# A prologue on one core: sixteen C loads and four B loads issued from the sync queue, angles folded once on VectorE, parameters requested at piece 5

## The chip, the cores and the metric

The kernel runs on one core of a Trainium2 chip. The metric is the device time of one execution in microseconds (us). The core has five engines with a queue each: PE (TensorE, the matrix engine), DVE (VectorE), ACT (ScalarE), POOL (GpSimd) and SP (SyncE, which only issues transfers). ACT and POOL issue transfers too. Engines meet at semaphores.

## The reference

One inference step of a hybrid encoder layer over two groups of tokens: 1024 prompt tokens and 64 sample tokens (1088 in all), model width 2048, all in float32. The input is RMS-normalised and multiplied by `w_in`; the columns feed an S5 branch (64 groups of 16 channels, each driving 64 complex states) and a forgetting-attention branch (8 heads of 128). Both are gated, normalised, concatenated and multiplied by `w_out`. What matters here is the discretisation of the S5 parameters:

```python
dt = exp(log_dt)[:, None]
mag = exp(a_re * dt)
abar_re, abar_im = mag * cos(a_im * dt), mag * sin(a_im * dt)
den = a_re * a_re + a_im * a_im
nr, ni = abar_re - 1.0, abar_im
coef_re, coef_im = (nr * a_re + ni * a_im) / den, (ni * a_re - nr * a_im) / den
bb_re = coef_re * (u @ b_re) - coef_im * (u @ b_im)
bb_im = coef_re * (u @ b_im) + coef_im * (u @ b_re)
# h[t] = abar * h[t-1] + bb[t];  y = c_re . h_re - c_im . h_im + d * u
```

The kernel needs powers 1 to 8 of `abar` and the angles of six further powers, hence 14 multiples of `a_im * dt` for 4096 states: a tile `arg` of 128 x 448, whose cosines and sines go to `trg` (2 x 448 columns).

## The kernel before

It has three parts: a prologue, the S5 part and, after a barrier of all engines, the attention, gate and output part. The change touches the prologue and the start of the S5 part.

**Prologue.** The tokens come as nine tiles `m` = 0 to 8 of 128 rows (the last has 64), 1 MB each. SP loads them (L333, L339); tiles 4 to 8 reuse the place of an earlier one and wait (`X_FREE`) until PE has transposed it (`x_t`). Per tile, ACT squares and sums it in four instructions (`x_square`, L399), DVE reduces the four sums (L568), ACT takes the root (L405), DVE inverts it and scales the tile (L571 to L578), PE transposes it (`tiles`, L960), ACT writes the high part `XH` (`x_split`, L411) and DVE the rest `XL` (`x_rest`, L586). On ACT the order in step m is `x_square(m+1)`, `x_split(m)`; on DVE it is `x_scale(m+1)`, `x_rest(m)`. PE transposes tile m+1 only when `x_rest(m)` has released the PSUM banks. PE also computes the gate columns after tiles 3, 6 and 8 (`gate`, L973), and transposes C after tiles 5 and 6 (`turn_c`, L982; DVE takes it with `take_c`, L593).

ACT's queue also issues transfers: eleven for the parameters at the start, and behind `x_split(m)` of steps 0 to 4 four each: the sixteen `load_c` of 32 KB (L385, rows of 256 bytes) and the four `load_b` of 128 KB (L390, rows of 64 bytes).

POOL works on the parameters in one long chain, each instruction waiting for the one before: `exp_poly` for dt (L783 to L796, 32 columns), the multiples `arg` (L807), the fold of the angles into -pi to pi, once for the cosine and once for the sine (L815 to L825, 10 and 9 instructions of 448 columns), `mag` (L832), `exp_poly` on 256 columns, then, after ACT's sine (L430, `trg_sin`), the packing of `pk` (L840 to L874). L882 stores `pk` to DRAM (`st_pk`).

**Start of the S5 part.** PE streams weight pieces: `w_in` comes in pieces of 256 rows x 128 columns into `wraw` (L167), ACT makes `whi` (L172), DVE makes `wlo` (L176), and PE multiplies each with all tokens in 18 matmuls of three column groups (L188). A column tile of 128 output columns has 8 pieces. ACT and DVE prepare piece s+4 in step s. At step `BEGIN` = 3 both first wait for `st_pk`, DVE clears three tiles (L746 to L748), and ACT then issues the load of the parameters `PJ` of group block 0 (L545). One step later DVE builds `DC` and `BD` (`prepare`, L627 to L632) and half of `Q` (`prepare_q(0)`, L642 to L645), two steps later the other half (L648 to L651). In step 7 (`HP - 1`) DVE and ACT take the finished column tile out of PSUM (`take_u`, L656, L450). POOL builds `GR` from `PJ` (L894 to L899, `g_ready`), which PE must transpose (L1000) before piece 8; after piece 8 PE transposes the tile U (`st1`, L1024), for which it waits for ACT's and DVE's copies `LS` (L459, L666). From there the loop over blocks j runs.

Of the kernel before, what the change touches and what calls it, by code (L numbers as in the profile page):

```python
# [24 lines left out]
NG, GC, NP = 64, 16, 64  # L25
D_PROJ = 2 * D_SSM + 4 * D_ATT + NH
EPS = 1e-6
P = 128
# [18 lines left out]
MAGIC = 12582912.0  # L47
# [3 lines left out]
def build_kernel(nc, x_prompt, x_sample, cache_k, cache_v, cache_logf, state_ssm_re, state_ssm_im,  # L51
# [12 lines left out]
    def sem(name):  # L64
        if name not in sems:
            sems[name] = nc.alloc_semaphore(name=f"{name}_{phase[0]}")
        return sems[name]
# [55 lines left out]
    with ctx:  # L123
# [86 lines left out]
        with ExitStack() as st:  # L210
# [12 lines left out]
            wki = sbp("wki", [P, 256], i32)  # L223
            cf = sbp("cf", [P, 8, 32])
            wg = sbp("wg", [P, KT, 2 * NH], r32)
            pk = sbp("pk", [P, 8, PKW])
# [30 lines left out]
        def x_all(m):  # L257
# [8 lines left out]
        ident_done, par_t, par_ev, dt_bc = sem("ident_done"), sem("par_t"), sem("par_ev"), sem("dt_bc")  # L266
        sq_done, xs_done, x_t, x_hi, x_lo = (sem(n) for n in ("sq_done", "xs_done", "x_t", "x_hi", "x_lo"))
        sqrt_done, ssq_v, trg_in, trg_sin, c_t, c_ev, pk_done = (
            sem(n) for n in ("sqrt_done", "ssq_v", "trg_in", "trg_sin", "c_t", "c_ev", "pk_done"))
# [3 lines left out]
        with ExitStack() as st:  # L273
# [27 lines left out]
            NJ = 8  # L301
            BEGIN = 3
            HP = KT // PIECE
# [26 lines left out]
            with nc.Block() as block:  # L330
                @block.sync
                def _(sp):
                    sp.dma_start(x_all(0), x_prompt[0, 0:P].rearrange("p (k c) -> p k c", k=KT)).then_inc(ld_x[0], 16)  # L333
                    sp.dma_start(gain[:], norm_gain[0:1, :].to_broadcast([P, D_MODEL])).then_inc(ld_gain, 16)
                    for m in range(1, TT):
                        if m in X_FREE:
                            sp.wait_ge(x_t, 4 * (X_FREE[m] + 1))
                        src = x_prompt[0, m * P:(m + 1) * P] if m < TT - 1 else x_sample[0]
                        sp.dma_start(x_all(m), src.rearrange("p (k c) -> p k c", k=KT)).then_inc(ld_x[m], 16)  # L339
                        if m == 1:  # L340
                            sp.dma_start(wf, w_in_v[:, :, D_PROJ - NH:D_PROJ]).then_inc(ld_wf, 16)
# [24 lines left out]
                def _(act):  # L366
# [14 lines left out]

                    def load_c(i):
                        a = (ssm_c_re, ssm_c_im)[i // 8]
                        q, g = i % 8 // 2, i % 2
                        act.dma_start(cin[:, i // 2, g * NP:(g + 1) * NP], a[0].rearrange("(q r g) c p -> q g r c p", q=4, g=2)[q, g]).then_inc(ld_c, 16)  # L385

                    def load_b(i):
                        a = (ssm_b_re, ssm_b_im)[i // 2]
                        g = i % 2
                        act.dma_start(braw[g * NP:(g + 1) * NP, i // 2].rearrange("p (r c) -> p r c", c=GC),  # L390
                                      a[0].rearrange("(r g) p c -> g p r c", g=2)[g]).then_inc(ld_b, 16)
                    act.wait_ge(ident_done, 2)
# [22 lines left out]
                    for m in range(TT):  # L415
                        if m + 1 < TT:
                            x_square(m + 1)
                        x_split(m)
                        if m == 0:
                            act.wait_ge(ld_wf, 16)  # L420
                            S.copy(wg[:, :, 0:NH], wf).then_inc(wg_hi, 1)
                        if m < 5:
                            for i in range(4 * m, 4 * m + 4):
                                if i < 16:
                                    load_c(i)
                                else:
                                    load_b(i - 16)
                        if m == 5:
                            act.wait_ge(trg_in, 1)
                            S.activation(trg[:].rearrange("p a b c -> p (a b c)"),  # L430
                                         trg[:].rearrange("p a b c -> p (a b c)"), ACT.Sin).then_inc(trg_sin, 1)
                        if m == 7:
                            for s in range(SPL):
                                W.split_hi(s, s, 1)
# [125 lines left out]
                def _(dve):  # L560
# [43 lines left out]
                    for m in range(TT):  # L604
# [6 lines left out]
                        if m == 2:  # L611
                            dve.wait_ge(den_in, 1)
                            V.reciprocal(cf[:, 6], cf[:, 2]).then_inc(den_rec, 1)
                        if m == 5:
                            take_c(0)
# [150 lines left out]
                def _(pool):  # L766
                    o = Order(pool, "pool_order")
                    G.memset(epsc[:], EPS)
                    o.then(G.memset(ident[:], 0.0))
                    o.then(G.affine_select(out=ident[:], in_=ident[:], compare_op=ALU.not_equal, fill=1.0, base=0,  # L770
# [37 lines left out]
                    pool.wait_ge(o.sem, last)  # L808

                    argf = arg[:].rearrange("p a b -> p (a b)")  # L810
                    C1, C2, C3 = 6.28125, 1.9350051879882812e-3, 3.0199159819567e-7
                    for i, quarter in ((0, 0.25), (1, 0.0)):
                        t, u = wk[:, 0], wk[:, 1]
                        r = trg[:, i].rearrange("p a b -> p (a b)")
                        o.then(G.tensor_scalar(t, argf, 1.0 / (2 * math.pi), quarter, ALU.mult, ALU.add))  # L815
                        o.then(G.tensor_scalar(t, t, MAGIC, -MAGIC, ALU.add, ALU.add))
                        o.then(G.tensor_scalar(u, t, -C1, None, ALU.mult))
                        o.then(G.tensor_tensor(r, u, argf, ALU.add))
                        o.then(G.tensor_scalar(u, t, -C2, None, ALU.mult))
                        o.then(G.tensor_tensor(r, u, r, ALU.add))  # L820
                        o.then(G.tensor_scalar(u, t, -C3, None, ALU.mult))
                        o.then(G.tensor_tensor(r, u, r, ALU.add))
                        if quarter:
                            o.then(G.tensor_scalar(r, r, math.pi / 2, None, ALU.add))
                        ins = G.tensor_scalar(r, r, -3.1415925, 3.1415925, ALU.max, ALU.min)  # L825
                        if quarter:
                            o.then(ins)
                        else:
                            ins.then_inc(trg_in, 1)
                    pool.wait_ge(trg_in, 1)  # L830
                    for k in range(8):
                        last = o.step(G.tensor_scalar(mag[:, k + 1], ath[:, 0], float(k + 1), None, ALU.mult))  # L832
                    pool.wait_ge(o.sem, last)
                    o.then(G.tensor_copy(xm, mag[:, 1:9].rearrange("p a b -> p (a b)")))
                    exp_poly(mag[:, 1:9].rearrange("p a b -> p (a b)"), xm, 256)
# [1134 lines left out]
```

## Time and profile before

| | |
|---|---|
| median of 3 runs | 2177.96 us (2173.99 to 2178.43) |
| the profiled execution | 2175.9 us, of which the span of the profile is 2174.3 us |
| mean granted TensorE clock | 0.977 of full speed |
| PE busy | 2055.3 us, 95% of the span |
| DVE, ACT, POOL busy | 45%, 33%, 24% |
| prologue: first piece of the weight stream on PE | 94.43 us after the start of the span |
| `st1` transposes of block 0 (L1024), from which the loop runs | 136.53 us |

The page gives busy times and the groups of instructions; the timeline lists instructions in order of time with the idle time of the engine before each and what released it (in brackets); the table of waits sums such idle times by who waited for whom. SPq, ACTq and POOLq are the queues' own instructions, such as issuing a transfer.

### The profile page before, as it was taken

The page shows a single profiled execution, that of the slowest core. Times are in us where ns is not written, and L with a number is a line of the kernel's source. Part 1 is how long each engine was busy: PE and PEld are TensorE (multiplying, and loading weights), DVE is VectorE, ACT ScalarE, POOL GpSimd, SP SyncE. Part 2 cuts the span into 40 slices and gives each one's busy share as a digit, 9 for nine tenths or more (in the row PEclk, how much of TensorE's full clock was granted, in tenths as well). Part 3 has the DMA queues.
Part 4 walks back from the last instruction along what each step waited for, and adds up shares of the span by engine and source line. Part 5 has one row for each costly group of instructions (what it writes and reads, how often), then busy time and mean ns, then how long its engine had stood idle before and what let it go on. Part 6 is the DMA issues. An engine that isn't in the chain of part 4 may idle for free.

```text
span 2174.3 us, 36318 instructions
## 1 busy us (share of the span) xinstructions
PE 2055.3 (95%) x12932; PEld 1966.9 (90%) x12932; DVE 973.6 (45%) x1795; ACT 708.2 (33%) x1458; POOL 519.3 (24%) x771
## 2 busy tenths in 40 slices
PE   4789999999969999999999999999999889999997
PEld 3579999999969999999999999999988879999997
DVE  6454555555533334342524444352564553333332
ACT  5413332333333233333333333334365531111110
POOL 6964555444500001010010101001022212222222
PEclk8799999999989999999999999999999989999999
DMA  6222222222122212112121212112173533333222
GB/s 189 45 68 65 69 69 58 59 69 69 51 57 57 62 32 80 33 43 70 33 81 31 81 31 76 36 44 68 47 265 114 154 98 85 91 87 90 82 84 56
DMA packets 194779, 162.17 MB, mean 75 GB/s; under 512 B 26755, under 2 KB 176429, under 8 KB 193381
## 3 DMA queue, kind: packets, MB, share of 16 engines
q1 hardware_dynamic: 163984, 97.89, 17.2%
q0 software_dynamic: 14704, 51.19, 7.8%
q10 hardware_dynamic: 16036, 12.39, 1.8%
q8 instruction: 31, 0.51, 0.1%
q14 instruction: 24, 0.19, 0.0%
HBM read 124.47 MB, written 36.95 MB: 74 GB/s over the span
## 4 chain that ended last, share of the span: by engine, by line
PE 65%; DMA 2%; DVE 2%; issue 1%; ACT 1%; POOL 0%; SPq 0%; DVEq 0%; POOLq 0%; ACTq 0%
PE GB L188 46%; PE TB L188 9%; PE TB L1781 3%; PE TB L1802 3%; PE TB L1843 1%; PE TB L1826 1%; PE TB L1898 1%; PE TB L1858 1%; DMA ys_s<-QR 1%; DVE QR L1538 0%; DVE QR L1536 0%; DMA out_k_sample<-KO 0%; DMA XL<-ys_s 0%; ACT whi L172 0%; DMA KO<-zs_s 0%
## 5 line engine op out<-in xcount | busy, mean ns | idle before, releaser
L188 PE MATMUL GB<-XH,whi 128*128 128x384 f32 (+1 forms) x2880 | 970.4, 337 | 28.6 <-DVE wlo L176 16.7
L188 PE MATMUL GB<-XH,wlo 128*128 128x384 f32 (+1 forms) x2880 | 947.7, 329 | 0.0
L188 PE MATMUL GB<-XL,whi 128*128 128x384 f32 (+1 forms) x2880 | 945.1, 328 | 0.0
L176 DVE TENSOR_TENSOR wlo<-wraw,whi 128x256 fp32r<-128x256 f32 x544 | 265.9, 490 | 830.1 <-ACT whi L172 826.5
L188 PEld LDWEIGHTS GB<-XH,whi 128*128 128x128 f32 x2880 | 545.8, 190 | 45.0 <-issue 23.6
L188 PEld LDWEIGHTS GB<-XL,whi 128*128 128x128 f32 x2880 | 545.9, 190 | 0.0
L188 PEld LDWEIGHTS GB<-XH,wlo 128*128 128x128 f32 x2880 | 544.7, 189 | 0.0
L172 ACT CAST whi<-wraw 128x256 fp32r<-128x256 f32 x544 | 219.5, 405 | 992.3 <-PE GB L188 811.7
L1247 POOL DMA_DIRECT2D ya_s<-ZR x7 | 4.1, 579 | 750.7 <-DVE ZR L1610 750.7
L1637 DVE RECIPROCAL SQ<-SQ 128x136 f32<-128x136 f32 x128 | 127.7, 997 | 1.1
L188 PE MATMUL TB<-XH,wlo 128*128 128x384 f32 (+1 forms) x384 | 126.0, 328 | 0.0
L188 PE MATMUL TB<-XH,whi 128*128 128x384 f32 (+1 forms) x384 | 125.7, 327 | 0.0
L188 PE MATMUL TB<-XL,whi 128*128 128x384 f32 (+1 forms) x384 | 125.6, 327 | 0.0
L1437 ACT ACTIVATE PR<-PR,nmx 128x128 f32<-128x128 f32 (+8 forms) x72 | 53.4, 742 | 165.2 <-DVE nmx L1623 165.2
L1345 ACT ACT_TABLE_LOAD x64 | 82.1, 1283 | 1.1
L1781 PE MATMUL TB<-PT,VT 128*128 128x128 f32 x576 | 74.7, 275 | 0.7 <-ACT PT L1447 0.7
L1781 PEld LDWEIGHTS TB<-PT,VT 128*128 128x128 f32 x576 | 71.3, 191 | 1.3 <-ACT PT L1447 1.2
L1802 PE MATMUL TB<-KN,QN 128*128 128x512 f32 (+2 forms) x192 | 72.5, 486 | 0.0
L188 PEld LDWEIGHTS TB<-XH,whi 128*128 128x128 f32 x384 | 72.1, 188 | 0.1
L188 PEld LDWEIGHTS TB<-XH,wlo 128*128 128x128 f32 x384 | 72.2, 188 | 0.0
L188 PEld LDWEIGHTS TB<-XL,whi 128*128 128x128 f32 x384 | 72.1, 188 | 0.0
L1621 DVE CUSTOM_DVE_ANT_0 PR<-TB,NCB 128x128 f32<-128x128 f32 (+8 forms) x72 | 51.2, 711 | 39.4 <-PE TB L1803 35.9
(389 smaller groups left out, 2182.7 us busy)
## 6 DMA issues: line engine op xcount, KB each, us to landing
wraw<-in_w_in SPq DMA_DIRECT2D x384, 128.0 KB, 2.2
wraw<-in_w_out SPq DMA_DIRECT2D x128, 128.0 KB, 2.2
xt<-in_x_prompt SPq DMA_DIRECT2D x5, 1024.0 KB, 5.0
NCB<-nc_s POOLq DMA_DIRECT2D x8, 608.0 KB, 5.3
zg_s<-U ACTq DMA_DIRECT2D x8, 544.0 KB, 2.8
XL<-zg_s SPq DMA_DIRECT2D x8, 544.0 KB, 4.6
VR<-zg_s POOLq DMA_DIRECT2D x8, 544.0 KB, 4.6
KO<-zs_s POOLq DMA_DIRECT2D x8, 544.0 KB, 5.9
```

What stands on the lines that cost most here:

```text
L172: S.copy(whi[:, s % SPL], wraw[:, s % RAW]).then_inc(self.hi, 1)
L176: V.tensor_tensor(wlo[:, s % SPL], wraw[:, s % RAW], whi[:, s % SPL].bitcast(f32), ALU.subtract).then_inc(self.lo, 1)
L188: ins = T.matmul(group(GB if bank is None else bank, b), w[:, s % SPL, kk], x[:, k + kk, c:c + n], start=first and kk == 0 and i == 0, sto ...
L1345: o.then(S.activation(tabs[:], epsc[:], func))
L1437: S.activation(PR[0:n, 0:w], PR[0:n, 0:w], ACT.Exp, bias=nmx[0:n], accum_out=rsum[0:n]).then_inc(e["exp"], 1)
L1621: o.then(V.tensor_tensor_reduce(out=PR[0:n, 0:w], in0=TB[0:n, 0:w], in1=NCB[0:n, c:c + w], scale=1.0, scalar=-3e38, op0=ALU.add, op1=ALU.m ...
L1637: o.then(V.reciprocal(a, a))
L1781: ins = T.matmul(O, VT[:, b], PT[:, b * P:(b + 1) * P], start=b == 0, stop=b == i)
L1802: T.matmul(TB[:, c:c + cw], q, KN[:, c:c + cw], start=True, stop=c + cw < w)
L1826: ins = T.transpose(TB[:, 1024 + b * P:1024 + (b + 1) * P], PR[:, b * P:(b + 1) * P], ident[:])
L1843: ins = T.matmul(TB[:, d:d + n], ones[:], SQ[:, c:c + n], start=True, stop=True)
L1858: ins = T.transpose(TB[0:n, d:d + P], src[:, m * P:m * P + n], ident[:])
```

## The change

- `load_c` and `load_b` move from ACT's queue to SP's: C loads 0 to 7 in front of the load of tile 4, 8 to 15 in front of tile 5, the four B loads in front of tile 6.
- POOL no longer folds the angles. It signals `arg_done` after L807, computes `mag` and then waits for DVE's fold (`trg_in`). DVE folds once, in six instructions of 448 columns, behind `x_rest(3)`.
- In step 5 ACT takes the absolute value of the folded angle and then the cosine as sin(pi/2 - |angle|), and the sine, in three instructions where there was one of 896 columns. A new constant `halfpi` is set by POOL.
- `BEGIN` goes from 3 to 5.

```diff
-            BEGIN = 3
+            BEGIN = 5
@@ sync queue
+                    (load_c and load_b as on ACT's queue before, with sp.dma_start)
                     for m in range(1, TT):
+                        if m in (4, 5):
+                            for i in range(8 * (m - 4), 8 * (m - 3)):
+                                load_c(i)
+                        if m == 6:
+                            for i in range(4):
+                                load_b(i)
                         if m in X_FREE:
                             sp.wait_ge(x_t, 4 * (X_FREE[m] + 1))
@@ scalar queue
-                        if m < 5:
-                            for i in range(4 * m, 4 * m + 4):
-                                if i < 16:
-                                    load_c(i)
-                                else:
-                                    load_b(i - 16)
                         if m == 5:
                             act.wait_ge(trg_in, 1)
-                            S.activation(trg[:].rearrange("p a b c -> p (a b c)"),
-                                         trg[:].rearrange("p a b c -> p (a b c)"), ACT.Sin).then_inc(trg_sin, 1)
+                            tf = lambda i: trg[:, i].rearrange("p a b -> p (a b)")
+                            S.activation(tf(0), tf(1), ACT.Abs).then_inc(trg_abs, 1)
+                            act.wait_ge(trg_abs, 1)
+                            S.activation(tf(0), tf(0), ACT.Sin, bias=halfpi[:], scale=-1.0)
+                            S.activation(tf(1), tf(1), ACT.Sin).then_inc(trg_sin, 1)
@@ vector queue, behind x_rest(m)
+                        if m == 3:
+                            dve.wait_ge(arg_done, 1)
+                            argf = arg[:].rearrange("p a b -> p (a b)")
+                            t, r = trg[:, 0].rearrange("p a b -> p (a b)"), trg[:, 1].rearrange("p a b -> p (a b)")
+                            o.then(V.tensor_scalar(t, argf, 1.0 / (2 * math.pi), MAGIC, ALU.mult, ALU.add))
+                            o.then(V.tensor_scalar(t, t, -MAGIC, None, ALU.add))
+                            o.then(V.scalar_tensor_tensor(r, t, -6.28125, argf, ALU.mult, ALU.add))
+                            o.then(V.scalar_tensor_tensor(r, t, -1.9350051879882812e-3, r, ALU.mult, ALU.add))
+                            o.then(V.scalar_tensor_tensor(r, t, -3.0199159819567e-7, r, ALU.mult, ALU.add))
+                            V.tensor_scalar(r, r, -3.1415925, 3.1415925, ALU.max, ALU.min).then_inc(trg_in, 1)
@@ gpsimd queue
+                    G.memset(halfpi[:], math.pi / 2)
@@
-                    (the two folds, L810 to L829)
-                    pool.wait_ge(trg_in, 1)
+                    pool.sem_inc(arg_done, 1)
                     for k in range(8):
                         last = o.step(G.tensor_scalar(mag[:, k + 1], ath[:, 0], float(k + 1), None, ALU.mult))
                     pool.wait_ge(o.sem, last)
+                    pool.wait_ge(trg_in, 1)
                     o.then(G.tensor_copy(xm, mag[:, 1:9].rearrange("p a b -> p (a b)")))
```

## Rows read from the trace of the kernel before

**Rows 1.** The page: busy us, share of the span and instructions by engine.

```profile
PE 2055.3 (95%) x12932; PEld 1966.9 (90%) x12932; DVE 973.6 (45%) x1795; ACT 708.2 (33%) x1458; POOL 519.3 (24%) x771
```

**Rows 2.** PE's waits, 0 to 150 us: total, times, longest.

```profile
PE TB L960 <- DVE XL L586: 28.8, 7, 7.8
...
PE GB L188 <- DVE wlo L176: 4.2, 1, 4.2
```

**Rows 3.** ACT's waits, 0 to 150 us.

```profile
ACT TB L399 <- issue: 12.0, 5, 6.3
```

**Rows 4.** Timeline of DVE in the prologue: start, length, instruction, idle before it.

```profile
26.17 0.16 DVE L568 TENSOR_REDUCE ssq<-ssq 128x1 f32<-128x4 f32 x1 [2.77 <-ACT TB L399]
...
29.83 2.48 DVE L586 TENSOR_TENSOR XL<-TB,XH 128x512 fp32r<-128x512 f32 x4
...
47.67 0.15 DVE L568 TENSOR_REDUCE ssq<-ssq 128x1 f32<-128x4 f32 x1
...
59.50 0.16 DVE L568 TENSOR_REDUCE ssq<-ssq 128x1 f32<-128x4 f32 x1 [5.05 <-ACT TB L399]
...
71.06 0.16 DVE L568 TENSOR_REDUCE ssq<-ssq 128x1 f32<-128x4 f32 x1 [3.70 <-ACT TB L399]
```

**Rows 5.** Timeline of ACT and its queue in the prologue.

```profile
20.92 0.30 ACT L421 CAST wg<-pk 128x128 fp32r<-128x128 f32 x1
...
49.22 3.99 ACTq L390 DMA_DIRECT2D braw<-in_ssm_b_re  x1
...
56.48 0.60 ACT L399 ACTIVATE TB<-XHF 128x512 f32<-128x512 f32 x1 [6.31 <-issue]
...
62.03 1.28 ACT L430 ACT_TABLE_LOAD   x1
67.20 0.95 ACT L430 ACTIVATE trg<-trg 128x896 f32<-128x896 f32 x1 [3.89 <-POOL trg L825]
```

**Rows 6.** Timeline of POOL: multiples of the angle, `mag`, end of the packing.

```profile
30.81 6.40 POOL L807 TENSOR_SCALAR arg<-ath 128x32 f32<-128x32 f32 x14
...
67.25 2.63 POOL L832 TENSOR_SCALAR mag<-ath 128x32 f32<-128x32 f32 x8
...
109.98 1.29 POOL L874 TENSOR_TENSOR pk<-wk,trg 128x512 f32<-128x512 f32 x1
```

**Rows 7.** Timeline of SP's queue.

```profile
3.07 8.33 SPq L339 DMA_DIRECT2D XHF<-in_x_prompt  x1
11.44 2.06 SPq L339 DMA_DIRECT2D XLF<-in_x_prompt  x1
```

**Rows 8.** The view of one tile: issue of C loads (ns min/median/max).

```profile
L385 ACTq DMA_DIRECT2D XLF<-in_ssm_c_im x8: 602/603/1295, 34.2 to 42.9; - x8
```

**Rows 9.** The view of tile xt: issue to landing of its six loads.

```profile
DMA to landing us min/median/max: 4.8/5.3/10.3
```

**Rows 10.** Timeline of PE: tile 4 behind the gate, and the start of the stream.

```profile
46.11 2.36 PE L960 MATMUL TB<-ident,xt 128*128 128x128 f32 x16
...
94.43 0.34 PE L188 MATMUL GB<-XH,whi 128*128 128x384 f32 x1
...
129.46 1.97 PE L1000 MATMUL TB<-ident,M 128*128 128x128 f32 x8 [5.26 <-POOL M L899]
...
136.53 0.27 PE L1024 MATMUL TB<-ident,UZ 128*128 128x128 f32 x1
```

**Rows 11.** Timeline of DVE at the start of the stream.

```profile
117.42 0.15 DVE L746 MEMSET UC<- 128x112 f32 x1 [12.08 <-DMA pk_s<-pk]
...
120.40 0.45 DVE L627 COPY DC<-PJ 128x548 f32<-128x548 f32 x1 [0.50 <-DMA PJ<-pk_s]
...
134.62 0.68 DVE L666 COPY LS<-TB 128x512 f32<-128x512 f32 x1
```

**Rows 12.** Timeline of DVE: durations of instructions on 548 columns.

```profile
157.12 0.72 DVE L698 TENSOR_TENSOR SS<-M 128x548 f32<-128x548 f32 x1
...
179.60 0.42 DVE L627 COPY DC<-PJ 128x548 f32<-128x548 f32 x1
```

More of the change, by code:

```diff
@@ L224, in build_kernel @@
             cf = sbp("cf", [P, 8, 32])
+            halfpi = sbp("halfpi", [P, 1])
             wg = sbp("wg", [P, KT, 2 * NH], r32)
@@ L267, in build_kernel @@
         sq_done, xs_done, x_t, x_hi, x_lo = (sem(n) for n in ("sq_done", "xs_done", "x_t", "x_hi", "x_lo"))
+        arg_done, trg_abs = sem("arg_done"), sem("trg_abs")
         sqrt_done, ssq_v, trg_in, trg_sin, c_t, c_ev, pk_done = (
@@ L334, in _, with load_c, load_b @@
                     sp.dma_start(gain[:], norm_gain[0:1, :].to_broadcast([P, D_MODEL])).then_inc(ld_gain, 16)
-                    for m in range(1, TT):
+                    def load_c(i):
+                        a = (ssm_c_re, ssm_c_im)[i // 8]
+                        q, g = i % 8 // 2, i % 2
+                        sp.dma_start(cin[:, i // 2, g * NP:(g + 1) * NP], a[0].rearrange("(q r g) c p -> q g r c p", q=4, g=2)[q, g]).then_inc(ld_c, 16)
+                    def load_b(i):
+                        a = (ssm_b_re, ssm_b_im)[i // 2]
+                        g = i % 2
+                        sp.dma_start(braw[g * NP:(g + 1) * NP, i // 2].rearrange("p (r c) -> p r c", c=GC),
+                                      a[0].rearrange("(r g) p c -> g p r c", g=2)[g]).then_inc(ld_b, 16)
+                    for m in range(1, TT):
+                        if m in (4, 5):
[4 more added lines that the diff above has]
+                                load_b(i)
                         if m in X_FREE:
@@ L380, in _ @@
                     act.dma_start(vin[33:34], k_norm_gain).then_inc(ld_par, 16)
[L382 to L391, printed above, removed]
                     act.wait_ge(ident_done, 2)
@@ L808, in _ @@
                     pool.wait_ge(o.sem, last)
[L810 to L829, printed above, removed]
-                    pool.wait_ge(trg_in, 1)
+                    pool.sem_inc(arg_done, 1)
                     for k in range(8):
```

## Prediction

> **What bounds the kernel now.** I read the page first: PE is busy 95% of the span [rows 1], nearly all of it the matmuls L188, which this change doesn't touch. So only time in which PE stands still, or does little, can be won, and the change can move that only in the first 140 us. There I read PE's waits [rows 2]: 28.8 us in seven waits for DVE's `XL` in the prologue, and 4.2 for `wlo` after the stream has begun; PE then waits 5.26 for POOL's `GR` [rows 10]. The prologue ends where the first piece starts, at 94.43, and the loop is entered at `st1`, at 136.53 [rows 10]. Everything behind `st1` is a stream that PE feeds itself; I take its length as unchanged. The question is thus by how much `st1` comes earlier.
>
> What sets the prologue's pace is a ring: DVE reduces tile m+1, scales it, makes `XL` of tile m; ACT meanwhile takes the root, splits tile m and squares tile m+2. Write t(m) for the start of the reduce of tile m. DVE alone needs 29.83 + 2.48 - 26.17 = 6.14 a tile [rows 4]. ACT needs 2.53 from the reduce to the end of the split (59.50 to 62.03) and 3.02 for the squares (56.48 to 59.50) [rows 4, 5], 5.55 together, so DVE should be the slower one. But the steps really took longer: t(5) 47.67, t(6) 59.50, t(7) 71.06 [rows 4]. ACT's waits say why: 12.0 us in five places behind "issue" [rows 3], the largest being 6.31 ahead of the squares of tile 6, behind the B loads [rows 5], and 3.89 before the sine, for POOL's fold [rows 5]. DVE's idle times before the reduces, 2.77, 5.05 and 3.70, are the same delays seen from its side [rows 4].
>
> **The change, part by part.**
>
> *Loads leave ACT.* ACT is free of tile 0 and `wg` at 20.92 + 0.30 = 21.2 [rows 5]; it squares tile 2 at once: t(2) = 21.2 + 3.1 = 24.3 (before 26.17). Then DVE's 6.14 rules: t(3) = 30.4, t(4) = 36.6 (a small reciprocal in step 2 is left out).
>
> *Loads on SP.* Twenty issues now stand in front of loads of tokens. SP has issued tile 3 at 13.5 [rows 7]. At 0.60 each [rows 8] C loads 0 to 7 take until 18.3, ahead of the time at which tile 4 may be asked for (20.4, when tile 0 has been transposed). C loads 8 to 15 follow, 20.8 to 25.6; tile 5 is issued at 25.6 and lands 5.3 later [rows 9], at 31. Its squares are due behind the split of tile 3, at t(4) + 2.5 = 39.1: covered with 8 us to spare. The four B loads took ACT's queue 7.9 us in all, the second one 3.99 [rows 5]; on SP, 26 to 34. Tile 6 is issued at 34 and lands by 39.3, or by 44.3 with the longest landing, 10.3 [rows 9]. It is due at t(5) + 2.5 = 48.6. So I cost the moved issues at nothing; the cover is 4 to 9 us. The bound from the other side: at 1.30 a C load, the longest one [rows 8], tile 5 lands at about 40 (1 late), tile 6 at 52 (3 late). Tiles 7 and 8 are asked for when tiles 4 and 5 are transposed, as before, and rows of C and B no longer stand near them.
>
> *The fold.* POOL has the multiples ready at 30.81 + 6.40 = 37.2 [rows 6]; DVE comes to the fold behind `x_rest(3)`, at t(4) + 6.1 = 42.7, so it waits for nothing. Six instructions of 448 columns: three with one tensor, priced 0.42, and three with two, priced 0.72 [rows 12]; both rows are of 548 columns and I leave the surplus for the six hand-overs. 3.4 us; the bounds are 2.8 (scaled to 448 columns) and 5.0 (all at 0.72, and 0.1 for each hand-over). Queued behind it on DVE: the reduce of tile 5, so the whole 3.4 lies on the ring. t(5) = 42.7 + 3.4 = 46.1 (before 47.67). PE transposes tile 4 behind the gate columns, 2.2 earlier than its 46.11 [rows 10], which is early enough for the split. t(6) = 46.1 + 6.1 + 0.5 = 52.7 (before 59.50); the 0.5 is for POOL's `exp_poly`, which now runs beside it.
>
> *Sine and cosine.* In step 5 ACT waits no more (fold ready 46.1). It does root and split (2.5), the absolute value (0.6 with its hand-over), the table load (1.28), two sines of 448 columns (1.1; one of 896 took 0.95) and the squares of tile 7 (3.0) [rows 4, 5]: t(7) = 52.7 + 8.5 = 61.2 against 71.06. ACT sets this step; DVE would need 6.1 + 0.7 for `take_c`. From t(7) to the first piece nothing changes, 94.43 - 71.06 = 23.4 [rows 4, 10]: the stream starts at 84.6, 9.8 earlier.
>
> A rule of the Trainium skill bears on the absolute value: "ScalarE: Activation LUTs", section "Table sets: the hidden batching unit", says that cheap functions, abs among them, are in every table set. By it no further load appears; no row here shows the absolute value, and one more load would cost 1.28, the length of the one in the row [rows 5], and put the stream at 85.9.
>
> *POOL's chain.* Without the folds it has `mag` done at 37.2 + 2.6 = 39.8 and waits for DVE until 46.1. From there to the end of `pk` it has what stood between 67.25 + 2.63 = 69.9 and 109.98 + 1.29 = 111.3, 41.4 us [rows 6]: 87.5. The sine is there at 58, long before. The store took from 111.3 to 117.4 [rows 6, 11]: `st_pk` at 93.6, while the stream reaches step 5 of its preparation five pieces after its start. A piece takes 2.98 us (the matmuls of the stream before the stall ran at that pace, as 94.43 plus eight times 2.98 plus the 4.2 wait and a slow restart of 1.7 give 124.2, 5.26 before 129.46) [rows 2, 10]. DVE clears at 84.6 + 14.9 + 1.3 = 100.8; the wait for `st_pk` has vanished with 7 us to spare, and with it the 4.2 and the slow restart.
>
> *BEGIN = 5.* But now `PJ` is asked for at 100.8, by choice and not by need. It is there 120.40 - 117.42 = 3.0 later [rows 11], 103.8. POOL made `GR` in 129.46 - 120.40 = 9.1 [rows 10, 11]; DVE was at work beside it, which it now is only for the second half, so 8.0 to 9.1, I take 8.5: 112.3. PE has finished piece 7 at 84.6 + 23.9 = 108.5: it waits 3.8 for `GR`. It transposes it (1.6) and multiplies piece 8 (3.9, with a cold start): 117.8. DVE starts `prepare` behind `wlo` of piece 10, at 106.4. Before, it went from 120.40 to 134.62 + 0.68 = 135.3, 14.9 us, from there to its copy of `LS` [rows 11], two `wlo` more than now: 14.0, bounds 10.5 (its copies unhindered by POOL) and 14.9. `LS` is ready at 120.4, and `st1`, which waits for both, starts at 120.4 against 136.53: 16.1 us earlier. `take_u` now stands ahead of the second half of `Q`, which removes the wait for it in piece 8, and `LS` behind it becomes what is late: 2.6 us.
>
> The sum: 9.8 from the prologue, 6.3 from the start of the stream, 16.1. The profiled execution took 2175.9, 2.1 below the median of 2177.96 and within the spread of the runs: 2175.9 - 16.1 = 2159.8, or 2161.9 from the median. I say 2161.
>
> **Rivals.**
>
> *Tokens late (2).* C at 1.3 an issue and a fold at 5.0 cost 3 + 1.6, and if DVE's preparation stays at its upper bound 1 more: 16.1 - 5.6 = 10.5 gained, 2166. The margins of 4 to 9 us speak against it.
>
> *The queue fills (slower).* SP was held 8.33 us by one load of tokens behind four others [rows 7]. If each B load holds SP that long, in front of tile 6, four take 33.3. With C at 1.3 tile 6 is issued at 35 + 33.3 = 68.3 and lands at 73.6; t(6) = 76.6, the stream starts at 76.6 + 8.5 + 23.4 = 108.5, `st1` at 144.3, 7.8 later: 2185. It decides from t(6) = 68.6 on (52.7 + 16.1), that is if tile 6 is issued after 60.3. For it: SP's row. Against: the same four loads took ACT 7.9 us while tokens were moving too. The Trainium skill, "DMA: Bandwidth & Descriptors", section "Queues, rings and completion order", has a rule against the move: an engine takes descriptors of one ring in order and goes round robin between rings. By it the load of tile 6 has all of B before it, where on ACT's ring B ran beside tokens; no row here shows the two orders apart, and it would only lengthen the landing that I bounded at 10.3.
>
> *Only the start is won (the change doesn't do what it says).* If ACT's "issue" idle is not the transfers' but that of something which stays, or the fold on DVE costs the ring what ACT gains, the stream starts where it did. Then only the 6.3 remain: 2171; with 2 us of further waits in the loop, no measurable change, 2175. Against: the five places are exactly the five steps with loads.
>
> **How the numbers follow.** Forecast 0.66 (gain 13 to 19, the upper end from DVE's 10.5 and a `GR` in 8.0), tokens late 0.13, only the start 0.14 (half of it under the bound), slower 0.07. About 0.2%, 4.4 us, can be told from no change. Faster 0.86, same 0.07, slower 0.07. The range takes the first two cases, most of the third and the spread of the runs: 2155 to 2172.
>
> **What would show it.** After: no "issue" idle before L399; t(5) near 46 and t(6) near 53; the six folds within 3.4; two sines and one table load; first piece of the stream near 84.6; no wait for `st_pk`; a wait of about 4 for `GR` and one of 2 to 3 for `LS`; `st1` near 120. It is wrong if SP's B loads take over 15 us, if a tile's squares wait for its load, if DVE waits for `arg_done`, or if the loop behind `st1` grows.

## The result, and the profile after

The changed kernel takes 2159.81 us (median of 4 runs, 2158.79 to 2160.54) against 2177.52 of the kernel before (4 runs): the ratio is 0.9924, with a 95% interval of 0.9908 to 0.9939. The profiled execution took 2158.79 us with a span of 2157.2, against 2175.9 and 2174.3, so 17.1 us less. Forecast were 16.1 less, 2161 us. Run once more on another occasion, beside other kernels, the changed kernel took 2161.5 (ratio 0.9929, 0.9916 to 0.9943).

PE's matmuls are the same, as the page shows (busy us, share, instructions):

```profile
PE 2056.0 (95%) x12932; PEld 1967.2 (91%) x12932; DVE 972.2 (45%) x1801; ACT 708.6 (33%) x1460; POOL 494.3 (23%) x753
```

PE's waits of the changed kernel, 0 to 160 us, answer to [rows 2]. The seven waits for `XL` of 28.8 us are six of 18.9, the one for `wlo` is gone, and what is left at the start of the stream is 2.9 for `GR`, 0.8 for `take_u` and 0.2 in front of `st1`:

```profile
PE TB L956 <- DVE XL L591: 18.9, 6, 4.6
...
PE TB L996 <- POOL M L895: 2.9, 1, 2.9
...
PE GB L188 <- DVE UZ L671: 0.8, 1, 0.8
```

The ring on DVE, from its timeline, answers to [rows 4]. The reduces are t(2), t(3), t(4), t(5), t(6) and t(7); between t(4) and t(5) lie the fold's first and last instruction:

```profile
23.95 0.16 DVE L573 TENSOR_REDUCE ssq<-ssq 128x1 f32<-128x4 f32 x1 [0.53 <-ACT TB L407]
...
30.09 0.14 DVE L573 TENSOR_REDUCE ssq<-ssq 128x1 f32<-128x4 f32 x1
...
36.47 0.10 DVE L573 TENSOR_REDUCE ssq<-ssq 128x1 f32<-128x4 f32 x1
...
42.48 0.38 DVE L623 TENSOR_SCALAR trg<-arg 128x448 f32<-128x448 f32 x1
...
45.30 0.39 DVE L628 TENSOR_SCALAR trg<-trg 128x448 f32<-128x448 f32 x1
...
45.61 0.15 DVE L573 TENSOR_REDUCE ssq<-ssq 128x1 f32<-128x4 f32 x1
...
51.82 0.15 DVE L573 TENSOR_REDUCE ssq<-ssq 128x1 f32<-128x4 f32 x1
...
60.17 0.16 DVE L573 TENSOR_REDUCE ssq<-ssq 128x1 f32<-128x4 f32 x1 [1.45 <-ACT TB L407]
```

DVE sets the pace nearly everywhere: it is idle before only two of these reduces, 0.5 and 1.5 us, where it had been idle before five of the six, for 2.8, 0.3, 1.6, 5.1 and 3.7. The stretches up to t(6) are 6.1 to 6.4 long, but for the one with the fold, 9.14; the last, 8.35, is set by ACT.

ACT in step 5, in its timeline: absolute value, table load, cosine, sine, then at once the squares of tile 7. This answers to [rows 5], where ACT had waited 3.89 us after the table load:

```profile
54.24 0.58 ACT L433 ACTIVATE trg<-trg 128x448 f32<-128x448 f32 x1
54.84 1.28 ACT L435 ACT_TABLE_LOAD   x1
56.13 0.67 ACT L435 ACTIVATE trg<-trg,halfpi 128x448 f32<-128x448 f32 x1
56.70 0.56 ACT L436 ACTIVATE trg<-trg 128x448 f32<-128x448 f32 x1
```

SP's queue, with the moved loads in it. The rows answer to [rows 7] and to the B loads of [rows 5]:

```profile
13.89 7.75 SPq L340 DMA_DIRECT2D XLF<-in_ssm_c_re  x8
21.68 0.45 SPq L357 DMA_DIRECT2D xt<-in_x_prompt  x1
22.18 6.05 SPq L340 DMA_DIRECT2D XLF<-in_ssm_c_im  x8
28.27 0.45 SPq L357 DMA_DIRECT2D xt<-in_x_prompt  x1
28.76 4.40 SPq L345 DMA_DIRECT2D braw<-in_ssm_b_re  x2
33.20 3.15 SPq L345 DMA_DIRECT2D braw<-in_ssm_b_im  x2
36.40 1.51 SPq L357 DMA_DIRECT2D XHF<-in_x_prompt  x1
```

PE's timeline at the start of the stream, which answers to [rows 10]: the first piece at 83.92 instead of 94.43, the transposes of `GR`, and `st1` at 118.65 instead of 136.53:

```profile
83.92 0.34 PE L188 MATMUL GB<-XH,whi 128*128 128x384 f32 x1
...
110.83 1.10 PE L996 MATMUL TB<-ident,M 128*128 128x128 f32 x8 [2.92 <-POOL M L895]
...
118.65 0.35 PE L1020 MATMUL TB<-ident,UZ 128*128 128x128 f32 x1 [0.22 <-issue]
```

So 10.5 us are won in front of the stream and 7.4 between its first piece and `st1` (34.7 instead of 42.1), 17.9 in all; the span is shorter by 17.1. The rest of 0.8 lies behind `st1`: from there to the end of the span the kernel before takes 2037.8 us and the changed one 2038.6. The thirteen profiled executions of this document take between 2036.7 and 2042.4 us for that stretch, so 0.8 is not a change that can be told.

### The profile page after: what moved, and what is told of

Read it like the earlier page. It is cut to its first block, busy times and chain, and to the rows that moved or that the text cites. A ratio compares the mean times of both kernels' runs of the same rounds, so it can differ in the third digit from the quotient of the medians.

```text
span 2157.2 us, 36310 instructions
## 1 busy us (share of the span) xinstructions
PE 2056.0 (95%) x12932; PEld 1967.2 (91%) x12932; DVE 972.2 (45%) x1801; ACT 708.6 (33%) x1460; POOL 494.3 (23%) x753
## 4 chain that ended last, share of the span: by engine, by line
PE 65%; DVE 2%; DMA 2%; issue 1%; ACT 1%; POOL 0%; SPq 0%; DVEq 0%; POOLq 0%; ACTq 0%
PE GB L188 45%; PE TB L188 9%; PE TB L1777 3%; PE TB L1798 3%; PE TB L1839 1%; PE TB L1822 1%; PE TB L1894 1%; DMA ys_s<-QR 1%; PE TB L1854 1%; DMA out_k_sample<-KO 0%; DVE QR L1534 0%; DVE QR L1532 0%; DMA XL<-ys_s 0%; DMA KO<-zs_s 0%; ACT whi L172 0%
## 5 line engine op out<-in xcount | busy, mean ns | idle before, releaser
L188 PE MATMUL GB<-XH,whi 128*128 128x384 f32 (+1 forms) x2880 | 968.3, 336 | 24.6 <-DVE wlo L176 12.0
L188 PE MATMUL GB<-XH,wlo 128*128 128x384 f32 (+1 forms) x2880 | 946.7, 329 | 0.0
L188 PE MATMUL GB<-XL,whi 128*128 128x384 f32 (+1 forms) x2880 | 943.8, 328 | 0.0
L188 PEld LDWEIGHTS GB<-XH,whi 128*128 128x128 f32 x2880 | 544.9, 189 | 40.7 <-issue 24.1
L188 PEld LDWEIGHTS GB<-XL,whi 128*128 128x128 f32 x2880 | 545.1, 189 | 0.0
L188 PEld LDWEIGHTS GB<-XH,wlo 128*128 128x128 f32 x2880 | 544.0, 189 | 0.0
L188 PE MATMUL TB<-XH,wlo 128*128 128x384 f32 (+1 forms) x384 | 125.8, 328 | 0.0
L188 PE MATMUL TB<-XH,whi 128*128 128x384 f32 (+1 forms) x384 | 125.6, 327 | 0.0
L188 PE MATMUL TB<-XL,whi 128*128 128x384 f32 (+1 forms) x384 | 125.5, 327 | 0.0
L188 PEld LDWEIGHTS TB<-XH,whi 128*128 128x128 f32 x384 | 72.1, 188 | 0.1
L188 PEld LDWEIGHTS TB<-XH,wlo 128*128 128x128 f32 x384 | 72.1, 188 | 0.0
L188 PEld LDWEIGHTS TB<-XL,whi 128*128 128x128 f32 x384 | 72.0, 188 | 0.0
```

Of the source, the lines that this page charges most:

```text
L188: ins = T.matmul(group(GB if bank is None else bank, b), w[:, s % SPL, kk], x[:, k + kk, c:c + n], start=first and kk == 0 and i == 0, sto ...
```

## The experiments

In what follows two figures stand for each kernel: the start of the stream (first matmul L188) and how long after it `st1` begins, both from its profiled execution, and the median of its runs. Kernel before: 94.4, 42.1, 2177.5. Changed: 83.9, 34.7, 2159.8. The seven profiled executions whose prologue is that of the changed kernel start the stream at 83.9 to 85.1, so a difference of 1 us there is not read as an effect; the distance to `st1` is 34.73 and 34.70 in the two executions of the changed kernel.

### One part alone: the loads

`e1_loads_only` is the kernel before with this part of the change only:

```diff
@@ scalar queue, step m
-                        if m < 5:
-                            (four of load_c or load_b)
@@ sync queue
+                        if m in (4, 5):
+                            for i in range(8 * (m - 4), 8 * (m - 3)):
+                                load_c(i)
+                        if m == 6:
+                            for i in range(4):
+                                load_b(i)
```

> The kernel before with one part of the change alone: C and B loads on SP. POOL still folds the angles, the sine is one instruction, BEGIN is 3. Theory (the prologue is a ring with due times, and the steps of ACT have two delays one behind the other): t(5) near 43 and t(6) near 50, both about 5 to 9 us earlier than the 47.7 and 59.5 of before, but in step 5 ACT then waits for POOL's fold, which ends near 67 as before, so t(7) is 71 and the stream starts at 94 again: time 2176 within 2 us, ACT's wait for POOL's fold grown from 3.9 to 11 to 14 us. Rival (the parts add up, each its own share of the 17 us): the 12.0 us of issue idle are what is won, the stream starts at 86 to 88 and the time is 2166 to 2169.

Measured: 2177.38 us, ratio 1.0 (0.999 to 1.001). The stream starts at 96.8 and `st1` at 136.2, 39.4 later. The ring is as early as the theory says up to t(6), and then loses it all, as DVE's timeline shows (t(4) to t(7)):

```profile
36.56 0.10 DVE L568 TENSOR_REDUCE ssq<-ssq 128x1 f32<-128x4 f32 x1
...
43.07 0.14 DVE L568 TENSOR_REDUCE ssq<-ssq 128x1 f32<-128x4 f32 x1
...
50.45 0.16 DVE L568 TENSOR_REDUCE ssq<-ssq 128x1 f32<-128x4 f32 x1 [1.25 <-ACT TB L405]
...
71.82 0.16 DVE L568 TENSOR_REDUCE ssq<-ssq 128x1 f32<-128x4 f32 x1 [14.64 <-ACT TB L405]
```

ACT's waits name the cause: the "issue" idle before the squares, 12.0 us [rows 3], does not appear any more, and what had been 3.9 for POOL's fold is now

```profile
ACT trg L430 <- POOL trg L825: 13.7, 1, 13.7
```

The parts do not add up; the loads alone are worth nothing. One thing I had not foreseen: the stream starts 2.4 us later than in the kernel before, though t(7) is only 0.8 later. PE's longest wait for `XL` was 11.5 us instead of 7.8, and its granted clock in the last gate columns (the 7 us before the stream) was 0.63, where it had been 0.76 in the last 6 us of the kernel before. That the lower clock is the whole of the difference was not tried.

### One part alone: the fold

`e2_fold_only` is the kernel before with the fold on DVE, the absolute value and the two sines; the loads stay on ACT and `BEGIN` is 3. Seen from the changed kernel:

```diff
-            BEGIN = 5
+            BEGIN = 3
@@ load_c and load_b back on ACT's queue, behind x_split(m), four a step
```

> The kernel before with the fold on DVE, the absolute value and two sines, and nothing else: loads on ACT, BEGIN 3. Theory: the prologue gains nothing, since the 3.1 us of fold lie on the ring and ACT's issue stays (t(7) near 71, stream at 94.5), but POOL is done with the parameters near 92 and not at 111, so the store is there before step 3 asks for it: the wait of 4.2 for wlo and the one of 5.3 for GR go, PE waits for take_u instead, 1 to 3 us; st1 near 125.5 against 136.5. Time 2165, 10 to 12 us faster. Rival (parts add up by the cost of what each removes on its own engine): POOL's 30 us are off the path of PE and the 3.1 us of DVE are on it, time 2176 to 2181.

Measured: 2163.2 us, ratio 0.9937 (0.9918 to 0.9956). The stream starts at 91.2 and `st1` comes at 123.5, 32.3 later; PE's waits for `wlo` and `GR` are gone, and 2.8 for `take_u` is in their place. The rival is out: POOL's fold did not stand on PE's path by its own 30 us, but the parameters that waited for it did. The theory missed one thing, and it is the 3 us by which the prologue did get shorter. The fold on DVE lay partly in time in which DVE had waited for ACT, and ACT's 3.9 for POOL was gone. DVE's idle times show it:

```profile
49.27 0.15 DVE L573 TENSOR_REDUCE ssq<-ssq 128x1 f32<-128x4 f32 x1
...
59.16 0.16 DVE L573 TENSOR_REDUCE ssq<-ssq 128x1 f32<-128x4 f32 x1 [3.60 <-ACT TB L401]
...
67.51 0.16 DVE L573 TENSOR_REDUCE ssq<-ssq 128x1 f32<-128x4 f32 x1 [1.09 <-ACT TB L401]
```

t(5) is later by 1.6 than in the kernel before, not by the 3.1 of the fold, and the idle time before t(6) fell from 5.05 to 3.60: the loads' issue hid the rest.

### One part alone: BEGIN

`e3_begin_only` is the kernel before with this line changed:

```diff
-            BEGIN = 3
+            BEGIN = 5
```

> The kernel before with BEGIN at 5. Theory: the store of the parameters lands at 117.4 as before, so PJ and GR come as before (GR at 129.5); PE has one piece more ready and does not wait for wlo, but it can't pass piece 8 without GR; take_u stands earlier in DVE's order. st1 near 134.5, 1 to 3 us earlier, time 2174 to 2176. Rival (BEGIN is what makes the gain at the start of the stream, 7 us): st1 near 129.5, time 2169.

Measured: 2176.1 us, ratio 0.9993 (0.9984 to 1.0003): no change that could be told. `st1` starts at 135.1, 1.4 earlier than before, as the theory has it, and 40.8 behind the stream's 94.4. PE's two waits have become one, as long as both and the third for `take_u` together (4.2, 5.3 and 1.4 before):

```profile
PE TB L1000 <- POOL M L899: 11.1, 1, 11.1
```

The sum of the three parts alone is 0 + 14 + 1 us by the medians; together they bring 17 to 18. What the loads are worth once the fold has left POOL is more than the remaining 3. `e4_begin3`, which follows, is `e2_fold_only` with the loads on SP and nothing else changed: 2158.03 us against 2163.2, so 5.2 less, with the first piece at 85.1 against 91.2 and `st1` at 117.7 against 123.5. `BEGIN` = 5, on the other hand, is worth 1 us alone and costs 2 us at `st1` beside the other two.

### BEGIN in the changed kernel

`e4_begin3` and `e5_begin4` are the changed kernel with only this line changed to 3 and to 4:

```diff
-            BEGIN = 5
+            BEGIN = 3
```

> The changed kernel with BEGIN back at 3. Theory: the store has landed at 96.8, while step 3 comes at 94: PJ is asked for at 97.1 instead of 100.2, GR is ready near 109 (DVE works beside POOL all the time), PE waits about 1 us for it and 2 to 3 for take_u; st1 near 116.8 against 118.65, time 2157, 1 to 2 us faster than the changed kernel. Rival (waiting for the store two pieces earlier holds ACT and DVE back, which is why BEGIN was moved): pieces 7 to 9 are late again, st1 at 122 to 125, time 2163 to 2166.

> The changed kernel with BEGIN at 4. Measured from the first piece of the stream, st1 came 34.7 us later in the changed kernel (BEGIN 5) and 32.6 with BEGIN 3. Theory (what is last is DVE's order: the whole of Q stands ahead of take_u as soon as BEGIN is below 5, and it starts 3 us later than with BEGIN 3): GR is ready when piece 7 ends, PE waits under 1 us for it, but 3.5 to 5 for take_u; st1 34 to 35 behind the first piece, time as that of the changed kernel within 1 us. Rival (what counts is only how early the parameters are asked for, and each step is worth the same): halfway between, 33.6, PE's waits in sum between 3.7 and 4.0.

Measured: with 3, 2158.03 us (ratio 0.9908, 0.9889 to 0.9928), `st1` 32.6 behind the first piece; with 4, 2159.93 (0.9917, 0.99 to 0.9933), 34.7 behind it. The medians are too near each other to rank; the traces do it. With 3, DVE waits 3.1 us for the store, which holds PE nowhere; PE waits 1.1 for `GR` and 2.9 for `take_u`; with 4 it waits for `take_u` alone, and that is the longest wait of the three kernels:

```profile
PE GB L188 <- DVE UZ L671: 5.0, 1, 5.0
```

So moving the request to step 5 was not needed once POOL was early, and what is last at this place is the order of DVE's work and not the time of the request: 3 is better by 2.1 us than 5, while 4 is no better.

### Is the fold on the ring? It is doubled

`e6_fold_twice` is the changed kernel with five of the six instructions done twice:

```diff
                             o.then(V.scalar_tensor_tensor(r, t, -3.0199159819567e-7, r, ALU.mult, ALU.add))
+                            (the same five instructions once more)
                             V.tensor_scalar(r, r, -3.1415925, 3.1415925, ALU.max, ALU.min).then_inc(trg_in, 1)
```

> The changed kernel with five of the six fold instructions on DVE done twice, one pass behind the other, 2.85 us more by their durations in the changed kernel's trace. Theory (the fold lies on the ring in full): t(5), t(7) and the first piece of the stream 2.8 later, time 2162.5, 2.5 to 3 us slower than the changed kernel. Rival (DVE has slack there, ACT or a load being late anyway): under 1 us.

Measured: 2162.12 us (ratio 0.993, 0.9913 to 0.9946), 2.3 over the changed kernel. From t(4) to t(5) it takes 11.98 us (36.67 to 48.65) against 9.14: 2.84 more on the ring, where the five instructions last 2.65 and their hand-overs the rest. The first piece starts at 87.4, against 83.9 to 85.1 without the second fold. The fold is paid in full on the ring; that the time grew by as much is likely, but its runs (2160.07 to 2166.03) overlap with those of the changed kernel.

### How much cover has the place in SP's queue?

`e7_all_ahead` is the changed kernel with all twenty loads in front of tile 4:

```diff
-                        if m in (4, 5):
-                            for i in range(8 * (m - 4), 8 * (m - 3)):
-                                load_c(i)
-                        if m == 6:
-                            for i in range(4):
-                                load_b(i)
+                        if m == 4:
+                            for i in range(16):
+                                load_c(i)
+                            for i in range(4):
+                                load_b(i)
```

> The changed kernel with all sixteen C and four B loads ahead of the load of tile 4 on SP. Theory (SP's order costs nothing only while a tile lands before its squares are due; B holds SP some 7.5 us and the tile behind it lands late): tile 4 is issued near 36 and lands near 45, its squares were due at 32.7, so t(4) moves from 36.5 to 48, tile 5 is less late than that, and from there the ring runs as before: stream at 94 to 96, time 2170 to 2172, 11 us slower than the changed kernel. Rival (the DMA engines have room and the place in SP's queue matters little): t(4) within 2 us of the changed kernel's, time 2160 to 2162.

Measured: 2164.82 us (ratio 0.9941, 0.9925 to 0.9958), 5.0 slower than the changed kernel, half of what was expected. Now ACT waits for a tile, 5.5 us, and the ring is late from t(4) on by 4.8 (ACT's wait, and t(4) on DVE):

```profile
ACT TB L406 <- DMA xt<-in_x_prompt: 5.5, 1, 5.5
```

```profile
41.26 0.16 DVE L572 TENSOR_REDUCE ssq<-ssq 128x1 f32<-128x4 f32 x1 [4.57 <-ACT TB L406]
```

The mechanism is there, the size was off, and SP's queue says where: the four B loads held it 4.9 us and not 7.5, so that tile 4 was issued at 32.05 and not at 36, and it was squared from 38.2 on, 6.2 us after its issue and not 9:

```profile
27.04 2.07 SPq L345 DMA_DIRECT2D braw<-in_ssm_b_re  x2
29.15 2.85 SPq L345 DMA_DIRECT2D braw<-in_ssm_b_im  x2
```

In the changed kernel a tile of 1 MB had been issued just ahead of the B loads; here only C loads of 32 KB stood ahead. That the megabyte is what makes the difference was not tried by itself.

### A better order

`e8_q_behind` is the changed kernel with `BEGIN` 3 and the second half of `Q` behind `take_u`:

```diff
-            BEGIN = 5
+            BEGIN = 3
@@ vector queue
-                        if s == BEGIN + 2:
+                        if s == HP - 1:
                             prepare_q(1)
```

> The changed kernel with BEGIN 3 and the second half of Q moved behind take_u on DVE, as BEGIN 5 has it by its place. Theory: PE's wait of 2.9 for take_u with BEGIN 3 goes to under 0.5, then LS is last by under 1 us; st1 31 to 31.5 behind the first piece (32.6 with BEGIN 3 alone, 34.7 in the changed kernel), time 2156 to 2157, the fastest of all. Rival (DVE's work is the same in sum, and LS comes behind all of it): the wait moves from take_u to LS and st1 stays at 32.5, time 2158.

Measured: 2157.14 us (ratio 0.9911, 0.9895 to 0.9928). The wait for `take_u` is gone and `st1` comes 31.4 behind the first piece, where `BEGIN` = 3 alone had 32.6; the medians of these two (2157.14 and 2158.03) are too near each other to rank. What is left ahead of `st1` is 1.8 for `LS` (the profile calls it issue; DVE's copy of `LS` ends just before):

```profile
109.77 1.09 PE L996 MATMUL TB<-ident,M 128*128 128x128 f32 x8 [1.53 <-POOL M L895]
...
115.67 0.35 PE L1020 MATMUL TB<-ident,UZ 128*128 128x128 f32 x1 [1.76 <-issue]
```

`e9_bd_on_act` adds one edit: the four copies of `BD` for block 0 go to ACT.

```diff
@@ scalar queue, behind split_hi of step BEGIN + 1
+                        if s == BEGIN + 1:
+                            act.wait_ge(e["pj_in"], 16)
+                            act.wait_ge(e["zero_done"], 3)
+                            for i in range(2):
+                                for g in range(2):
+                                    ins = S.copy(BD[i * NP:(i + 1) * NP, g::2, g * GC:(g + 1) * GC],
+                                                 bc_(i)[g * NP:(g + 1) * NP])
+                            ins.then_inc(e["bd_ready"], 1)
@@ vector queue
-                            prepare(0)
+                            prepare(0, bd=False)
```

It ran on one chip beside the changed kernel and `e8_q_behind`, each once more (`e11_q_behind_again` has the edit of `e8_q_behind`):

> The kernel with BEGIN 3 and the second half of Q behind take_u, and in addition the four copies that make BD for block 0 given to ACT, which waits at that place. Theory: DVE's way from PJ to LS is last there by 1.8 us, and the four small copies cost it 3.4 us because POOL works beside it; without them LS is ready before PE needs it, PE waits only for GR, 1 to 1.5 us; st1 29.3 to 30 behind the first piece of the stream (31.4 without this, 34.7 in the changed kernel), time 2155 to 2156. Rival (POOL and DVE only take turns: what DVE saves, POOL's GR or ACT's whi loses): st1 31 to 32, time 2157.

> The changed kernel once more, beside the two others, so that they are compared on one chip: 2158.5 to 2160.5.

> The kernel with BEGIN 3 and the second half of Q behind take_u once more: by its trace 2.5 to 3.3 us faster than the changed kernel on the same chip (st1 31.4 instead of 34.7 behind the first piece), 2156 to 2157.5; if the difference is under 1 us, what is won at st1 is given back in the loop.

Measured: 2154.91 (2153.3 to 2157.76; ratio 0.9905, 0.989 to 0.992), 2161.5 for the changed kernel (2158.79 to 2162.77) and 2155.96 for `e11_q_behind_again` (2153.56 to 2156.02; 0.9902, 0.9887 to 0.9917). The runs of the two new ones don't overlap with those of the changed kernel: 5.5 and 6.6 us faster (`e11_q_behind_again` and `e9_bd_on_act`). Of that the traces place 3.2 and 4.6 between the first piece and `st1`. The changed kernel itself came out 1 us above what was expected of it. Between the profiled executions of `e10_changed_again` and `e11_q_behind_again` all but 0.1 of the 5.5 us has a place: 0.55 in front of the stream, 3.2 up to `st1`, and 1.6 in the first 12 us behind `st1`, where PE's granted clock was low in the one and not in the other (see the last section). Of the 8.2 between the profiled executions of `e10_changed_again` and `e9_bd_on_act`, 1.7 lie further back and have no place. The two new ones cannot be ranked against each other. By the trace `BD` on ACT brings 1.4 us (30.1 against 31.5); PE still waits 1.3 for `GR` and 0.7 for `LS`. The expected 29.3 to 30 was just missed, because DVE did not save the 3.4: freed of the copies, its next instructions ran into POOL's. These rows of that kernel show it. In `e11_q_behind_again` the first of the products took 0.76, the second already 1.67, and the two `wlo` together 0.78. So 0.77 and 1.85 of the 3.4 came back; from `DC` to the end of `LS` DVE needed 14.0 us instead of 14.9. In the changed kernel the two products took 0.76 and 0.75; POOL was done with `GR` when they came:

```profile
101.12 1.53 DVE L667 TENSOR_TENSOR UC<-PJ 128x576 f32<-128x576 f32 x1
...
102.58 1.66 DVE L668 TENSOR_TENSOR UCS<-PJ 128x576 f32<-128x576 f32 x1
...
107.62 2.63 DVE L176 TENSOR_TENSOR wlo<-wraw,whi 128x256 fp32r<-128x256 f32 x2
```

## Why the prediction was right, point by point

- **The ring and its two stallers.** Forecast t(2) to t(7): 24.3, 30.4, 36.6, 46.1, 52.7, 61.2. Measured: 23.95, 30.09, 36.47, 45.61, 51.82, 60.17. The 6.14 a tile held. That ACT's "issue" idle was the loads' is shown by `e1_loads_only`, where it disappears with them; so the third rival's first half is out. That both stallers lay one behind the other, so that neither part alone could bring the 9.8, is shown by `e1_loads_only` (first piece 2.4 later), `e2_fold_only` (3.2 earlier) and `e4_begin3` (the two together, 9.3 earlier). The prediction worked both out together and did not say it.
- **Loads on SP at nothing.** The issue took longer than I said: C 7.75 and 6.05 us for eight instead of 4.8, so tile 5 was issued at 28.3 and not 25.6, and tile 6 at 36.4 and not 34. The cover of 4 to 9 us took that up: ACT waited for none of these tiles. The landing of tile 6 took 8.0 us from its issue, and 7.1 to 7.5 in the other eight profiled executions with this order; in the three with B on ACT's queue it took 6.9, 6.4 and 6.2. The rule that I quoted from the Trainium skill, "DMA: Bandwidth & Descriptors", section "Queues, rings and completion order", points the same way as these landings. That it is their cause is not shown, since the time counts from the start of the issue and the issue itself was 1.0 longer (1.51 against 0.55 in the kernel before). `e7_all_ahead` shows that the cover is real and what comes behind it, at a smaller price than I put on it. The slower rival had SP held 8.3 by each B load; held it was 7.5 by all four.
- **The fold.** 3.4 forecast. Six instructions took 3.04 by their durations, and from the first to the following reduce 3.13. `e6_fold_twice` shows it on the ring in full. On the ring the stretch became longer by 3.0 (9.14 against 6.14), between the bound of 2.8 from scaling the rows to 448 columns and the price I took.
- **Sine and cosine.** Forecast 8.5 from t(6) to t(7), measured 8.35. No table load came with the absolute value; the row goes from it straight to the load for the sine. By the Trainium skill, "ScalarE: Activation LUTs", section "Table sets: the hidden batching unit", abs is in every set; the trace agrees for the one set that was loaded then.
- **First piece.** Forecast 84.6, measured 83.9, and 85.0 in the repeated execution. In the first t(7) was 1.0 earlier than forecast, and the stretch behind it, which I had left as it was at 23.4, took 23.75.
- **POOL's chain.** Forecast end of `pk` 87.5; it was at 90.6. The term mis-sized is the stretch behind the fold, 41.4 forecast, 44.8 measured: four instructions of that stretch took over 2 us, where there had been two such in the kernel before; one product took 2.83 against 0.72 for its likes. That DVE's large instructions hold them is how I read it, and the rows fit closely: each of the four starts while DVE scales a tile (2.35 us) and ends 0.3 or 0.6 after that instruction, as if the most part of its usual 0.41 or 0.73 came behind it. No run takes the scaling away from them, so the cause is read and not tested. It cost nothing: the store was issued at 90.95 and, at 5.8 us to land, was there 3 us ahead of DVE's step 5 at 99.9.
- **BEGIN = 5.** Forecast: a wait of 3.8 for `GR` (2.9 measured), and `st1` 35.8 behind the first piece (34.7). The term mis-sized is DVE's way from `prepare` to `LS`, 14.0 forecast, 12.7 measured (105.84 to 118.55): POOL was done with `GR` at 110.8, and behind that the second product for `Q` took 0.75 and the pair that makes `Q` 1.52, where they had taken 1.66 and 3.27 beside POOL in the kernel before. `GR` itself, 8.5 forecast with a lower bound of 8.0, took 7.3 (103.46 to 110.78); with `BEGIN` = 3, where DVE's products for `Q` run beside it, it took 9.0 (101.00 to 109.97 in `e11_q_behind_again`). That this is what ends last I said, with PE's wait of 2.6 before it; in the profiled execution the wait was 0.2, in the repeated one 1.9, with the same 34.7. The difference is piece 8, priced at 3.9, which took 6.7 in the profiled execution at a granted clock of 0.56, with 0.8 for `take_u` in it. PE ended it at 118.43 and `LS` was ready at 118.55. That DVE was still last there is luck by 0.1 us, since the forecast had PE done 2.6 earlier.

The sum was 1.8 too small at `st1` and 1.0 in the profiled time. What the prediction did not weigh is whether the request at step 5 was needed at all. It said that it comes "by choice and not by need" and then priced what is there; `e4_begin3` and `e8_q_behind` show that 2 to 3 us were left there at `st1`.

## What to carry to other kernels

Where several engines pass a tile round in a ring, write down when each step is due and find every staller before pricing any: of two that stand one behind the other, taking one away can be worth nothing, and then be worth much once the other is gone (the loads: 0 us alone, 5.2 with the fold off POOL). Price a part in the kernel that has the others, and not by what the sum leaves over. A transfer's issue is cheapest in a queue that has slack before its next due time, and that slack can be measured by putting more in front. When a chain has become earlier, look again at the step at which its result is asked for, and at the order of work on the engine that ends last there: that was worth 3 us at `st1` for two lines, 2.7 by the medians in one comparison and 5.5 in the other.

## What the runs showed of the hardware

**The same loads hold a queue for different times.** Eight C loads of 32 KB took SP 7.75 and 6.05 us in the changed kernel though their median issue is 0.6; the view of the tile has the longest one:

```profile
L340 SPq DMA_DIRECT2D XLF<-in_ssm_c_re x8: 598/598/3224, 13.9 to 21.0; - x8
```

The four B loads held SP 7.5 us behind a tile of 1 MB (7.4 to 8.0 in the other eight executions with this order) and 4.9 behind C loads, which is one execution.

**A low clock that cost nothing in one execution and 1.6 us in another.** After the wait for `GR` the granted clock was 0.56 of full speed, mostly its lower level of 1.2 GHz, in the profiled execution of the changed kernel all through piece 8, and at its higher one in the repeated execution (stretch, length, busy us of PE, its weight loads, DVE, ACT and POOL, granted clock, transfers):

```profile
111.00:118.70 7.70, 6.67 (x27) 5.83 (x26) 7.36 (x11) 0.82 (x2) 6.83 (x19) 0.56 0.07 17
```

```profile
111.00:118.70 7.70, 4.30 (x26) 3.74 (x26) 7.51 (x11) 1.06 (x3) 6.84 (x16) 1.00 0.07 17
```

`st1` came 34.7 us behind the first piece in both, since DVE's `LS` was what ended last: the slow matmuls filled time in which PE would have waited. But in the repeated execution, where PE was busy for 4.3 of the 7.7 us at the higher level, the low one came 1 us behind `st1`, where PE has no wait to fill: granted clock 0.66 in the first 5 us, against 0.99 in the first execution (the columns as above):

```profile
118.65:123.65 5.00, 5.00 (x38) 4.63 (x42) 1.70 (x3) 1.29 (x4) 4.22 (x17) 0.99 0.14 33
```

```profile
119.66:124.66 5.00, 5.00 (x25) 4.64 (x26) 1.63 (x3) 1.05 (x2) 4.22 (x17) 0.66 0.14 33
```

The way from `st1` to the first 8x8 transposes (L1040) took 11.1 us there (and 11.2 in `e6_fold_twice` and `e7_all_ahead`, which have `BEGIN` = 5 too), but 9.5 in the first execution and in the three of `e8_q_behind`, `e9_bd_on_act` and `e11_q_behind_again`, whose granted clock was 1.00 on both sides of `st1`. So the better order, which leaves PE shorter waits, was free of this loss in all three of its profiled executions.

**DVE and POOL slow each other.** The small copies of `BD` took about 0.2 each where DVE came to them later in the loop (0.17 the first, 0.67 three together), and 0.8 to 0.97 at the start of the stream beside POOL's `GR`. Of POOL's six products for `GR` the last three took 1.19, 1.10 and 1.30 in the changed kernel, where DVE's products for `Q` came behind them, and 1.73, 1.63 and 1.66 in `e11_q_behind_again`, where they ran side by side; DVE's own took 0.75 and 1.67. Taking the copies off DVE moved the meeting to the next instructions and won 1.4 us of the 3.4.
